# Moving the mixer's RMSNorm into FFN1 and handing its result over through DRAM

## The chip, the cores and the metric

One Trainium2 chip, eight cores. Each core works on its own two sequences (4096 tokens) with the same program; nothing is exchanged between cores. The time is that of one execution on the device, in microseconds, of the slowest core.

## What is computed

One decoder layer on x (16 x 2048 x 1024, float32), bf16 in the matmuls:

```python
x = x + 0.5 * swiglu(rmsnorm(x, ffn1_norm), ffn1_w_gate, ffn1_w_up, ffn1_w_down)   # FFN1
h = rmsnorm(x, mix_norm)                                                           # the norm that moves
q_lat, kv_lat, k_rope, xc, gB, gC, gate_logits = split(h @ w_in)
y_a = causal_block_attention(q, k, v) @ w_proj_attn     # q, k, v from the latents
y_b = (gB * conv3(gC * xc)) @ w_proj_conv
gates = sigmoid(gate_logits + gate_bias)
x = x + (gates[..., :D] * y_a + gates[..., D:] * y_b) @ w_out                      # mixer
x = x + 0.5 * swiglu(rmsnorm(x, ffn2_norm), ffn2_w_gate, ffn2_w_up, ffn2_w_down)   # FFN2
```

D = 1024, the FFN width is 2816, 8 heads, sequence length 2048.

## The kernel before

**Tiling.** Tokens go in eight groups (g = 0 to 7) of 512, each of four tiles of 128. All eight groups pass FFN1, then the mixer, then FFN2. Between the stages x lies in DRAM as float32: `x1_d` after FFN1, `x2_d` after the mixer. The matmuls want the normed activations transposed, channel in the partitions; `hT[0]` and `hT[1]`, used by even and odd groups, hold one group each in bf16.

**Streams and planner.** The program is written as streams (generators) that yield operations, each with an engine, what it reads and writes, and a booked cost. `FW.schedule` merges them: it emits next the operation whose estimated start is earliest; ties go to the stream that stands earlier in the list. The order so found is fixed for each engine's queue, and engines execute in order. For a DMA it books 2 us plus the size at 310 bytes per ns (`DMA_FIX`, `DMA_RATE`), one after the other on SP; DMAs of other queues are not counted against it. `Wait` holds a stream back until a flag is set by a `Do` of another; flags are set when operations are emitted, not when they execute. All plain loads, stores and transposes are issued by SP; the casts of weights from float32 to bf16 in DRAM (`cast_w`, L853 and L863) by POOL.

**The norm.** `norm_stream` (L869 on) is used three times, for FFN1 (`f1`), the mixer (`m`) and FFN2 (`f3`). Per tile: a load to one of two `xin` buffers (L883), ACT's Square with a running sum (L901), two small POOL operations for the power -0.5 (L903, L905), DVE's multiply by the factor and the gain row `grow` into `xn` (L907), and a transposing DMA from `xn` to `hT` (L918). The load of tile n+1 is issued before tile n is normed. FFN1's first group is transposed by PE instead (L914).

**Gates.** FFN1's norm of group g (g of 2 or more) waits for `f1.gu.{g-2}`, the last gate/up matmul that reads the same hT. The mixer's norm loads tiles once FFN1's own norms are all emitted; group g of 0 and 1 waits for `f1.gu.{6+g}`, a later group for `d.h.{g-2}` (the last matmul of group g-2 that reads hT, in `proj`) and `m.q.{g-2}` (its latents). The norm buffers, the gain row and the DMA queue of SP are shared by the three uses.

**FFN1.** `ffn_stream`: for each group 22 pairs of gate and up matmuls (8 matmuls of 512 columns each), Silu on ACT (L957), product on DVE (L959), in rotation over four PSUM banks; then the down-projection of four tiles (L739 is the helper line of every matmul), the residual on DVE, the store to `x1_d` (L993) and the load of the next group's residual (L937). `f1.g.{g}` is set when the last of these is emitted. In group 0 all four tiles of the down-projection end together.

**Mixer.** Three streams run side by side: `m_stream` (latents, q, k, v of group g: `qkv`), `a_stream` (attention of group g) and `d_stream` (convolution, projections and output of group g: `conv`, `proj`, `outp`), the last with ten ring buffers of weights (`ring_stream`, L1240). `m.n.{g}` says that hT holds group g; `qkv(g)` and `conv(g)` wait for it.

Of the kernel before, what the change touches and what calls it, by code (L numbers as in the profile page):

```python
# [454 lines left out]
def c_stt(n):  # L455
    return 215.0 + n * 1.042
# [14 lines left out]
def build_program():  # L471
# [101 lines left out]
    def ffn_bufs(tag):  # L573
# [26 lines left out]
        for i in range(2):  # L600
            xr.append(mk(f"{tag}xr{i}", [D], F32, a, 2))
            a = xr[-1].end
        assert a <= HI, (a, HI)
        f.all = f.gu + f.sg + [f.act] + [f.wd] + xr
# [8 lines left out]
    commit_regs(f1.all)  # L613

# [85 lines left out]

    d_x1 = [[Dep(f"x1.{g}.{t}") for t in range(TPG)] for g in range(NG)]
    d_x2 = [[[Dep(f"x2.{g}.{t}.{h}") for h in range(2)] for t in range(TPG)] for g in range(NG)]
    d_out = Dep("out")
# [22 lines left out]
    s_tk = fw.new_dma_sem("tk")  # L726
    s_grow = fw.new_dma_sem("grow")
    s_set = [fw.new_dma_sem(f"set{i}") for i in range(5)]
# [12 lines left out]

    def ld_grow(i):
        return dma("sp", s_grow, lambda e: e.dma_start(out=grow.t[:], in_=row_d[0:1, i * D:(i + 1) * D].broadcast_to([128, D])),
                   [], grow.d, 128 * D * 4)

# [122 lines left out]

    def norm_stream(tag, src_d, srcdep, gi_, gate):  # L869
        work = [(g, tt) for g in range(NG) for tt in range(TPG)]  # L870
        first = tag == "f1"

        def xbuf(n):
            if first and n in (2, 3):
                ap, dd = f1.xr[n - 2]
                return ap, dd, s_xr[n - 2]
            return xin[n % 2].t[:], xin[n % 2].d, s_xin[n % 2]

        def load(n):
            g, tt = work[n]  # L880
            ap, dd, sem = xbuf(n)
            r0 = g * G + tt * 128
            return dma("sp", sem, lambda e: e.dma_start(out=ap, in_=src_d[r0:r0 + 128, :]), srcdep(g, tt), dd, 128 * D * 4)  # L883

        nl = 0
        yield Wait(gate(0, "x"))
        if not first:
            yield ld_grow(gi_)
        for n, (g, tt) in enumerate(work):
            if tt == 0:  # L890
                yield Wait(gate(g, "h"))
            while nl < len(work) and nl <= (3 if first and n == 0 else n + 1):
                yield Wait(gate(work[nl][0], "x"))
                yield load(nl)
                if first and nl == 0:
                    yield ld_grow(gi_)
                nl += 1
            i = n % 2
            h = hT[g % 2]
            xa, xd, _ = xbuf(n)  # L900
            yield op("act", lambda e, i=i, xa=xa: e.activation(out=xn[i].t[:], in_=xa, func=AF.Square, scale=1.0 / 32.0,  # L901
                                                               accum_out=ssq.t[:, i, 0:1]), xd, [xn[i].d, ssq.d[i]], c_act(1024) + 190)
# [3 lines left out]
                                                            op=ALU.pow), [ssq.d[i], nhalf.d], [rr.d[i]], c_pow(1))  # L906
            yield op("dve", lambda e, i=i, xa=xa: e.scalar_tensor_tensor(out=xn[i].t[:], in0=xa, scalar=rr.t[:, i, 0:1], in1=grow.t[:],  # L907
                                                                         op0=ALU.mult, op1=ALU.mult),
                     [xd, rr.d[i], grow.d], xn[i].d, c_stt(1024))
# [10 lines left out]
            yield Do(lambda n_=f"{tag}.t.{g}.{tt}": flags.add(n_))  # L920
            if tt == TPG - 1:
                yield Do(lambda n_=f"{tag}.n.{g}": flags.add(n_))

# [514 lines left out]

    def gate3(g, what):
        if what == "x":  # L1440
# [3 lines left out]
        return lambda: f"f3.gu.{g - 2}" in flags  # L1444

    streams = [
        setup_a(),
        norm_stream("f1", x_d, lambda g, t: [], 0, gate1),
        norm_stream("m", x1_d, lambda g, t: [d_x1[g][t]], 1, gate2),
        norm_stream("f3", x2_d, lambda g, t: d_x2[g][t], 2, gate3),  # L1450
        a_stream(),
# [40 lines left out]
```

## Time and profile before

| | us |
|---|---|
| median of 3 runs | 3209.21 |
| lowest of them | 3209.09 |
| the profiled execution | 3209.18 |
| its span, slowest core | 3207.6 |
| spans of the eight cores | 3187.7 to 3207.6 |
| PE busy in the span | 3089.6 |

The span runs from the first to the last instruction of the slowest core. PE is TensorE's matmuls, PEld its weight loads, DVE VectorE, ACT ScalarE, POOL GpSimd, SP the queue that issues DMAs. L901 is line 901 of the kernel printed above. In a timeline a bracket holds the idle time of the engine just before an instruction, and what ended it. A landing is the time from the issue of a DMA to its completion.

### The profile page before, as it was taken

To read this page: it belongs to the slowest core of one execution; us is meant where nothing else is said; L and a number is where in the kernel's file an instruction comes from. 1 tells how busy PE (TensorE), PEld (TensorE's weight loads), DVE (VectorE), ACT (ScalarE), POOL (GpSimd) and SP (SyncE) were. 2 spreads that over 40 slices of the span, in tenths; PEclk is the share of its full clock that TensorE was granted. 3 is DMA by queue.
4 is the path that set the end of the run, shared out by engine and by line. 5 is a ranking of instruction groups with operands and counts; after the bars stand their busy time and mean duration, and the time that the engine had idled before them with its cause. 6 is when DMAs were issued, how large, how long until landed. Compare 5 with 4: busy or idle time off the path is not lost.

```text
span 3207.6 us, 41366 instructions; the slowest of 8 cores (3187.7 to 3207.6 us)
## 1 busy us (share of the span) xinstructions
PE 3089.6 (96%) x14432; PEld 1407.8 (44%) x14432; DVE 1135.7 (35%) x1592; ACT 926.1 (29%) x1766; POOL 671.3 (21%) x1120
## 2 busy tenths in 40 slices
PE   7899999999999889999999999999999999999999
PEld 3344444444444344444444444444444444444444
DVE  4322221221236454554655554534222222122111
ACT  4311111111124434546343446363211111111100
POOL 1000000000026544342545343531100000000000
PEclk9999999999999999999999999999999999999999
DMA  9996564554425474756575656557670331131010
GB/s 314 296 129 141 137 100 107 132 118 92 127 66 144 101 190 108 192 129 160 141 205 138 199 124 164 145 145 242 170 223 21 92 92 34 59 92 53 27 53 27
DMA packets 333478, 419.32 MB, mean 131 GB/s; under 512 B 204896, under 2 KB 213216, under 8 KB 329696
## 3 DMA queue, kind: packets, MB, share of 16 engines
q1 hardware_dynamic: 325360, 380.83, 43.0%
q0 software_dynamic: 7920, 35.85, 7.6%
q8 instruction: 124, 2.03, 0.3%
q14 instruction: 74, 0.61, 0.1%
HBM read 355.45 MB, written 86.64 MB: 138 GB/s over the span
## 4 chain that ended last, share of the span: by engine, by line
PE 87%; DMA 4%; POOL 4%; DVE 3%; issue 1%; ACT 1%; SPq 0%; ACTq 0%; DVEq 0%; POOLq 0%
PE banks L739 87%; POOL hr L1117 1%; DMA xin_69<-x1s 1%; DVE Rs L1206 1%; DMA axr_105<-ws 1%; POOL qf L1128 1%; DVE T_109 L1093 1%; DVE hs L1095 0%; POOL mrgT L1377 0%; DMA xin_69<-x 0%; DMA QT_120<-qf 0%; DVE xn_71 L907 0%; DMA QT_136<-qf 0%; POOL hq L1119 0%; POOL kf L1135 0%
## 5 line engine op out<-in xcount | busy, mean ns | idle before, releaser
L739 PE MATMUL banks<-awd,aact 128*128 128x512 bf16 x1408 | 306.7, 379 | 4.9 <-ACT awd L830 3.8
L739 PE MATMUL banks<-cwd,cact 128*128 128x512 bf16 x1408 | 305.2, 379 | 0.0
L903 POOL TENSOR_SCALAR ssq<-ssq 128x1 f32<-128x1 f32 x96 | 25.6, 266 | 919.1 <-ACT xn_70 L901 825.2
L739 PEld LDWEIGHTS banks<-awd,aact 128*128 128x128 bf16 x1408 | 137.3, 98 | 171.7 <-issue 7.4
L739 PEld LDWEIGHTS banks<-cwd,cact 128*128 128x128 bf16 x1408 | 137.9, 98 | 166.0
L957 ACT ACTIVATE csg_173<-banks 128x512 f32<-128x512 f32 x88 | 52.5, 597 | 425.9 <-PE banks L739 425.9
L957 ACT ACTIVATE asg_94<-banks 128x512 f32<-128x512 f32 x88 | 52.5, 597 | 388.0 <-PE banks L739 388.0
L959 DVE TENSOR_TENSOR cact<-csg_173,banks 128x512 bf16<-128x512 f32 x88 | 60.5, 687 | 236.7 <-PE banks L739 236.7
L959 DVE TENSOR_TENSOR aact<-asg_94,banks 128x512 bf16<-128x512 f32 x88 | 60.6, 688 | 235.3 <-PE banks L739 235.2
L959 DVE TENSOR_TENSOR cact<-csg_174,banks 128x512 bf16<-128x512 f32 x88 | 60.5, 687 | 234.5 <-PE banks L739 234.5
L959 DVE TENSOR_TENSOR aact<-asg_95,banks 128x512 bf16<-128x512 f32 x88 | 60.5, 688 | 230.2 <-PE banks L739 227.9
L1183 ACT ACTIVATE pt_123<-banks 128x512 bf16<-128x512 f32 (+2 forms) x216 | 116.0, 537 | 86.6 <-PE banks L739 80.3
L1183 ACT ACTIVATE pt_124<-banks 128x512 bf16<-128x512 f32 (+2 forms) x214 | 113.6, 531 | 56.7 <-PE banks L739 51.7
L1183 ACT ACTIVATE pt_125<-banks 128x512 bf16<-128x512 f32 (+3 forms) x210 | 110.3, 525 | 58.1 <-PE banks L739 55.5
L957 ACT ACTIVATE csg_174<-banks 128x512 f32<-128x512 f32 x88 | 52.5, 597 | 252.3 <-PE banks L739 252.3
L1206 DVE RECIPROCAL Rs<-Rs 128x128 f32<-128x128 f32 x128 | 121.3, 948 | 11.0 <-ACT Rs L1200 9.2
L957 ACT ACTIVATE asg_95<-banks 128x512 f32<-128x512 f32 x88 | 52.5, 597 | 241.2 <-PE banks L739 238.4
L1117 POOL TENSOR_TENSOR hr<-hm,nhalf 128x8 f32<-128x8 f32 x64 | 111.0, 1734 | 4.7
L1202 DVE COPY Xo<-banks 64x512 f32<-64x512 f32 x64 | 44.0, 688 | 150.4 <-PE banks L739 97.7
L907 DVE SCALAR_TENSOR_TENSOR xn_71<-xin_69,rr,grow 128x1024 bf16<-128x1024 f32 x47 | 62.5, 1331 | 55.8 <-POOL rr L905 44.5
L901 ACT ACTIVATE xn_70<-xin_68 128x1024 bf16<-128x1024 f32 x47 | 49.5, 1052 | 112.0 <-DMA xin_68<-x 52.6
L907 DVE SCALAR_TENSOR_TENSOR xn_70<-xin_68,rr,grow 128x1024 bf16<-128x1024 f32 x47 | 62.8, 1335 | 51.9 <-POOL rr L905 37.0
(479 smaller groups left out, 5610.4 us busy)
## 6 DMA issues: line engine op xcount, KB each, us to landing
wms<-ws POOLq DMA_DIRECT2D x33, 512.0 KB, 5.0
ring_127<-wms SPq DMA_DIRECT2D x52, 256.0 KB, 3.1
ring_129<-wms SPq DMA_DIRECT2D x51, 256.0 KB, 3.2
ring_131<-wms SPq DMA_DIRECT2D x51, 256.0 KB, 3.0
ring_133<-wms SPq DMA_DIRECT2D x51, 256.0 KB, 3.0
ring_135<-wms SPq DMA_DIRECT2D x51, 256.0 KB, 3.1
ring_126<-wms SPq DMA_DIRECT2D x39, 256.0 KB, 3.3
ring_128<-wms SPq DMA_DIRECT2D x39, 256.0 KB, 3.5
```

The lines of the kernel that those rows point to most:

```text
L739: fns.append(lambda e, o_=o_, l_=l_, r_=r_, st=st, sp_=sp_: e.matmul(o_, lhsT=l_, rhs=r_, start=st, stop=sp_))
L901: yield op("act", lambda e, i=i, xa=xa: e.activation(out=xn[i].t[:], in_=xa, func=AF.Square, scale=1.0 / 32.0, accum_out=ssq.t[:, i, 0:1]) ...
L903: yield op("pool", lambda e, i=i: e.tensor_scalar(out=ssq.t[:, i, 1:2], in0=ssq.t[:, i, 0:1], scalar1=EPS, scalar2=1.0, op0=ALU.add, op1=A ...
L907: yield op("dve", lambda e, i=i, xa=xa: e.scalar_tensor_tensor(out=xn[i].t[:], in0=xa, scalar=rr.t[:, i, 0:1], in1=grow.t[:], op0=ALU.mult ...
L957: yield op("act", lambda e, s_=s_, b0=b0: e.activation(out=s_.t[:], in_=bk(b0), func=AF.Silu), [d_bank[b0]], s_.d, c_act(512))
L959: pend = op("dve", lambda e, s_=s_, b1=b1, c=c: e.tensor_tensor(out=f.act.t[:, c, :], in0=s_.t[:], in1=bk(b1), op=ALU.mult), [s_.d, d_bank ...
L1093: yield op("dve", lambda e: e.tensor_tensor(out=T1, in0=q2, in1=CQ.t[:, tt, None, :].broadcast_to([128, NH, 128]), op=ALU.mult), [d_bank[B ...
L1117: yield op("pool", lambda e, jj=jj: e.tensor_tensor(out=hr.t[:, b, jj], in0=hm.t[:, b, jj], in1=nhalf.t[:, 0:8], op=ALU.pow), [hm.d[dj], n ...
L1128: yield op("pool", lambda e: e.tensor_tensor(out=qf.t[:], in0=T1, in1=hq.t[:, b, 0:8, None].broadcast_to([128, NH, 128]), op=ALU.mult), [T ...
L1183: yield op("act", lambda e: e.activation(out=p_.t[:, 0:w], in_=bk(b0)[:, 0:w], func=AF.Exp, scale=sc), [d_bank[b0]], p_.d, c_act(w))
L1202: yield op("dve", lambda e: e.tensor_copy(out=X.t[po:po + 64, :], in_=bk(OB)[po:po + 64, :]), [d_bank[OB]], X.d, c_dve(512))
L1206: yield op("dve", lambda e, qs=qs: e.reciprocal(out=R.t[:, qs], in_=R.t[:, qs]), R.d, R.d, 80 + 6.4 * 128)
```

## The change

The mixer's norm becomes part of FFN1's norm stream. After FFN1's norm of group g+2 follow the four mixer tiles of group g: the x1 tile is loaded, normed with a gain row of its own (`grow2`), and the bf16 result is stored to a new DRAM tensor `h1_d` in place of the transpose. The mixer tiles of the last two groups follow at the end of the list. A new stream, `turn_stream`, waits for a group's norms to be emitted and for hT to be free (the old gates), and issues four transposing DMAs from `h1_d` to `hT`, each with a semaphore of its own. Mixer loads are gated by `f1.g.{g}`. Since the load of tile n+1 is yielded before tile n is normed, the fourth FFN1 tile of group g+2 also comes behind that gate. FFN2's norm stays as it was.

```diff
+    h1_d = nc.dram_tensor("h1s", [TOK, D], BF16).ap()
...
+        if tag == "a":
+            f.grow = mk("grow2", [D], F32, a)
...
-    def norm_stream(tag, src_d, srcdep, gi_, gate):
-        work = [(g, tt) for g in range(NG) for tt in range(TPG)]
+    def norm_stream(work, gate):
...
-            while nl < len(work) and nl <= (3 if first and n == 0 else n + 1):
-                yield Wait(gate(work[nl][0], "x"))
+            while nl < len(work) and nl <= (3 if startup and n == 0 else n + 1):
+                yield Wait(gate(work[nl][0], work[nl][1], "x"))
                 yield load(nl)
-                if first and nl == 0:
-                    yield ld_grow(gi_)
+                if startup and nl == 0:
+                    yield ld_grow(grow, 0)
+                if startup and nl == 4:
+                    yield ld_grow(grow2, 1)
                 nl += 1
...
-            if first and g == 0:
+            if tag == "m":
+                r0 = g * G + tt * 128
+                yield dma("sp", s_tx[i], lambda e, i=i, r0=r0: e.dma_start(out=h1_d[r0:r0 + 128, :], in_=xn[i].t[:]),
+                          xn[i].d, [d_h1[g][tt]], 128 * D * 2)
+            elif startup and g == 0:
...
+    def turn_stream(gate):
+        for g in range(NG):
+            yield Wait(lambda g=g: f"m.s.{g}" in flags)
+            yield Wait(gate(g))
+            for tt in range(TPG):
+                r0 = g * G + tt * 128
+                yield dma("sp", s_th[4 * (g % 2) + tt], lambda e, g=g, tt=tt, r0=r0: e.dma_start_transpose(
+                    out=hT[g % 2].t[:, :, tt * 128:(tt + 1) * 128], in_=h1_d[r0:r0 + 128, :]),
+                    [d_h1[g][tt]], [d_hT[g % 2][tt]], 128 * D * 2)
+            yield Do(lambda n_=f"m.n.{g}": flags.add(n_))
...
-    def gate1(g, what):
+    def gate1(tag, g, what):
+        if tag == "m":
+            return lambda: f"f1.g.{g}" in flags
         if what == "x":
             return lambda: "seta" in flags
         return lambda: g < 2 or f"f1.gu.{g - 2}" in flags
 
-    def gate2(g, what):
-        if what == "x":
-            return lambda: f"f1.g.{g}" in flags and f"f1.n.{NG - 1}" in flags
+    def gate2(g):
         if g < 2:
             return lambda: f"f1.gu.{NG - 2 + g}" in flags
         return lambda: f"d.h.{g - 2}" in flags and f"m.q.{g - 2}" in flags
...
+    tiles = range(TPG)
+    work1 = []
+    for g in range(NG + 2):
+        if g < NG:
+            work1 += [("f1", g, tt) for tt in tiles]
+        if g >= 2:
+            work1 += [("m", g - 2, tt) for tt in tiles]
...
-        norm_stream("f1", x_d, lambda g, t: [], 0, gate1),
-        norm_stream("m", x1_d, lambda g, t: [d_x1[g][t]], 1, gate2),
-        norm_stream("f3", x2_d, lambda g, t: d_x2[g][t], 2, gate3),
+        norm_stream(work1, gate1),
+        turn_stream(gate2),
+        norm_stream(work3, gate3),
```

## Rows read from the trace of the kernel before

**Rows 1.** The page: busy us of each engine; granted clock in 40 slices.

```profile
PE 3089.6 (96%) x14432; PEld 1407.8 (44%) x14432; DVE 1135.7 (35%) x1592; ACT 926.1 (29%) x1766; POOL 671.3 (21%) x1120
...
PEclk9999999999999999999999999999999999999999
```

**Rows 2.** Stages: length; PE, PEld, DVE, ACT, POOL busy; clock; DMA; GB/s.

```profile
0.00:153.00 153.00, 124.20 (x560) 54.53 (x560) 64.29 (x95) 61.37 (x82) 13.18 (x31) 0.98 1.01 311
153.00:960.00 807.00, 806.52 (x3742) 366.71 (x3743) 190.45 (x260) 129.32 (x233) 69.58 (x133) 1.00 0.56 116
960.00:1127.00 167.00, 148.48 (x699) 68.28 (x697) 95.53 (x137) 73.51 (x156) 100.33 (x154) 0.94 0.52 122
```

**Rows 3.** The same view: the six stretches in which mixer norms run.

```profile
1127.00:1167.00 40.00, 33.20 (x151) 15.26 (x150) 18.85 (x28) 19.45 (x43) 13.97 (x27) 0.87 0.97 231
...
1311.00:1351.00 40.00, 35.34 (x170) 16.32 (x169) 23.62 (x35) 19.47 (x45) 14.40 (x28) 0.96 0.87 226
...
1478.00:1518.00 40.00, 34.69 (x168) 16.37 (x167) 19.50 (x29) 24.76 (x57) 12.69 (x27) 0.96 0.88 215
...
1638.00:1678.00 40.00, 34.41 (x167) 15.89 (x165) 25.94 (x39) 16.41 (x39) 18.84 (x35) 0.91 0.94 246
...
1800.00:1840.00 40.00, 36.84 (x175) 16.87 (x174) 25.99 (x39) 14.96 (x36) 14.44 (x30) 0.96 0.92 259
...
1962.00:2002.00 40.00, 34.75 (x177) 16.52 (x175) 22.46 (x31) 24.55 (x56) 14.75 (x30) 1.00 0.86 231
```

**Rows 4.** The same view: the six stretches between and after them.

```profile
1167.00:1311.00 144.00, 135.79 (x642) 62.29 (x641) 69.33 (x100) 67.76 (x136) 61.71 (x98) 0.98 0.47 121
...
1351.00:1478.00 127.00, 125.25 (x601) 57.89 (x599) 60.29 (x88) 62.24 (x121) 53.92 (x80) 1.00 0.51 134
...
1518.00:1638.00 120.00, 117.26 (x568) 54.32 (x567) 65.39 (x95) 49.18 (x98) 59.55 (x91) 1.00 0.53 140
...
1678.00:1800.00 122.00, 116.01 (x562) 53.80 (x561) 65.70 (x93) 53.15 (x107) 58.08 (x90) 1.00 0.55 143
...
1840.00:1962.00 122.00, 117.57 (x559) 54.03 (x557) 56.47 (x83) 58.45 (x115) 56.12 (x82) 0.99 0.47 122
...
2002.00:2138.00 136.00, 131.73 (x624) 60.25 (x623) 65.87 (x93) 65.88 (x128) 55.72 (x84) 0.99 0.47 124
```

**Rows 5.** Timeline of the first norm in the mixer: start, us, instruction.

```profile
1127.65 0.38 SPq L883 DMA_DIRECT2D xin_69<-x1s  x1
...
1136.35 1.06 ACT L901 ACTIVATE xn_71<-xin_69 128x1024 bf16<-128x1024 f32 x1 [4.34 <-DMA xin_69<-x1s]
...
1138.12 0.48 PE L739 MATMUL banks<-QT_136,KT_137 128*128 128x384 bf16 x1 [4.27 <-ACT pt_124 L1183]
```

**Rows 6.** POOL's casts; SP's tile load at 172.78, its landing; a median landing.

```profile
168.93 1.12 POOL L853 DMA_DIRECT2D wms<-ws  x2 [43.35 <-ACT asg_95 L957]
...
172.78 0.53 SPq L883 DMA_DIRECT2D xin_69<-x  x1
...
DMA to landing us min/median/max: 31.9/31.9/31.9
...
xin_69<-x1s SPq DMA_DIRECT2D x16, 512.0 KB, 5.5
```

**Rows 7.** Timeline of ACT: a Silu beside gate/up; a Square beside down-projection.

```profile
178.40 0.60 ACT L957 ACTIVATE asg_94<-banks 128x512 f32<-128x512 f32 x1 [2.86 <-PE banks L739]
...
249.98 1.06 ACT L901 ACTIVATE xn_70<-xin_68 128x1024 bf16<-128x1024 f32 x1 [17.12 <-DMA xin_68<-x]
```

**Rows 8.** Page groups, multiply and Square: busy us, mean ns | idle before.

```profile
L907 DVE SCALAR_TENSOR_TENSOR xn_71<-xin_69,rr,grow 128x1024 bf16<-128x1024 f32 x47 | 62.5, 1331 | 55.8 <-POOL rr L905 44.5
...
L901 ACT ACTIVATE xn_70<-xin_68 128x1024 bf16<-128x1024 f32 x47 | 49.5, 1052 | 112.0 <-DMA xin_68<-x 52.6
```

**Rows 9.** Line 918, transposes: ns min/median/max on SP; landings of all 92.

```profile
L918 SPq DMA_TRANSPOSE hT_67<-xn_70 x24: 1216/1218/6082, 37.3 to 2949.5; - x24
...
DMA to landing us min/median/max: 3.1/4.0/14.1
```

More of the change, by code:

```diff
@@ L602, in ffn_bufs @@
             a = xr[-1].end
+        if tag == "a":
+            f.grow = mk("grow2", [D], F32, a)
+            a = f.grow.end
         assert a <= HI, (a, HI)
@@ L612, in build_program @@
             dp.until = f"f1.gu.{NG - 1}" if b in f1.gu else "f1.done"
-    commit_regs(f1.all)
+    grow2 = f1.grow
+    grow2.d[0].until = f"m.s.{NG - 1}"
+    commit_regs(f1.all + [grow2])
     m = Buf()
@@ L701, in build_program @@
     d_x1 = [[Dep(f"x1.{g}.{t}") for t in range(TPG)] for g in range(NG)]
+    d_h1 = [[Dep(f"h1.{g}.{t}") for t in range(TPG)] for g in range(NG)]
     d_x2 = [[[Dep(f"x2.{g}.{t}.{h}") for h in range(2)] for t in range(TPG)] for g in range(NG)]
@@ L726, in build_program @@
     s_tk = fw.new_dma_sem("tk")
-    s_grow = fw.new_dma_sem("grow")
+    s_grow = [fw.new_dma_sem(f"grow{i}") for i in range(3)]
+    s_th = [fw.new_dma_sem(f"th{i}") for i in range(8)]
     s_set = [fw.new_dma_sem(f"set{i}") for i in range(5)]
@@ L867, in build_program, with src @@
     xc_ = {}
-    def norm_stream(tag, src_d, srcdep, gi_, gate):
-        work = [(g, tt) for g in range(NG) for tt in range(TPG)]
-        first = tag == "f1"
+    def norm_stream(work, gate):
+        def src(n):
+            tag, g, tt = work[n]
+            r0 = g * G + tt * 128
+            if tag == "f1":
+                return x_d[r0:r0 + 128, :], []
+            if tag == "m":
+                return x1_d[r0:r0 + 128, :], [d_x1[g][tt]]
+            return x2_d[r0:r0 + 128, :], d_x2[g][tt]
+        startup = work[0][0] == "f1"
         def xbuf(n):
-            if first and n in (2, 3):
+            if startup and n in (2, 3):
                 ap, dd = f1.xr[n - 2]
@@ L879, in load @@
         def load(n):
-            g, tt = work[n]
             ap, dd, sem = xbuf(n)
-            r0 = g * G + tt * 128
-            return dma("sp", sem, lambda e: e.dma_start(out=ap, in_=src_d[r0:r0 + 128, :]), srcdep(g, tt), dd, 128 * D * 4)
+            sap, sd = src(n)
+            return dma("sp", sem, lambda e: e.dma_start(out=ap, in_=sap), sd, dd, 128 * D * 4)
         nl = 0
-        yield Wait(gate(0, "x"))
-        if not first:
-            yield ld_grow(gi_)
-        for n, (g, tt) in enumerate(work):
+        yield Wait(gate(work[0][0], 0, "x"))
+        if not startup:
+            yield ld_grow(grow, 2)
+        for n, (tag, g, tt) in enumerate(work):
             if tt == 0:
-                yield Wait(gate(g, "h"))
-            while nl < len(work) and nl <= (3 if first and n == 0 else n + 1):
-                yield Wait(gate(work[nl][0], "x"))
+                yield Wait(gate(tag, g, "h"))
+            while nl < len(work) and nl <= (3 if startup and n == 0 else n + 1):
+                yield Wait(gate(work[nl][0], work[nl][1], "x"))
                 yield load(nl)
-                if first and nl == 0:
-                    yield ld_grow(gi_)
+                if startup and nl == 0:
+                    yield ld_grow(grow, 0)
+                if startup and nl == 4:
+                    yield ld_grow(grow2, 1)
                 nl += 1
@@ L1437, in gate2, with gate3 @@
         return lambda: f"d.h.{g - 2}" in flags and f"m.q.{g - 2}" in flags
-    def gate3(g, what):
+    def gate3(tag, g, what):
         if what == "x":
```

19 lines of the change are left out of this document (11 added, 8 removed).

## Prediction

> **What bounds the kernel now.** The page's busy table comes first: PE is busy for 3089.6 of 3207.6 us, in 14432 matmuls [rows 1]. Whatever the change takes from other engines counts only where PE stands still or is slowed, so the second view is the stage table [rows 2]. FFN1 after its start-up (153 to 960 us) has no hole: 806.52 of 807 us, and 806.52 / 3742 = 0.2155 us a matmul. The start-up has 28.8 us of PE idle while the DMA engines are full (share 1.01). The passage into the mixer, 960 to 1127, loses 18.5 us idle, and its clock of 0.94 costs another 0.06 x 167 = 10 us.
>
> The third view is the same table for the mixer, cut at the places where it now does its norm. Tokens go in groups of 512, and the norms of groups 2 to 7 run when hT becomes free, at about 1127, 1311, 1478, 1638, 1800 and 1962 us [rows 3]; between them lie the six stretches of [rows 4]. I price a stretch as idle time plus (1 - clock) x length: a granted clock of 0.87 is a mean of 2.4 and 1.2 GHz. The six clusters lose 12.0, 6.3, 6.9, 9.2, 4.8 and 5.3 us, together 44.4. The stretches between lose 32.9 us in 771, or 1.7 per 40 us, so ordinary loss would be 10.2 and the excess at the norms is 34 us.
>
> The fourth view, the timeline of the first cluster, shows a mechanism [rows 5]. The load of an x1 tile is issued at 1127.65; ACT, which executes in order, stands at Square (L901) for 4.34 us until it has landed; the exponentials of attention stand behind Square, and PE waits 4.27 us for one of them. The excess is therefore mostly a queueing effect, not the 1.05 us of Square or the 1.33 us of the DVE multiply [rows 8].
>
> **What the change removes.** In the mixer go the x1 loads, Squares, POOL steps and DVE multiplies of groups 2 to 7: 24 tiles. I take 60 to 65% of the 34 us as gone, 22 us, since the same moments also contain the end of an attention head, merge adds on POOL and the first latent projections, which stay. Bounds: all 34, and 10 (about the waits like that of [rows 5], if the rest is merely re-timed).
>
> **What it adds in the mixer.** Per group four transposes from DRAM follow each other on SP: 4 x 1.22 = 4.9 us of issue [rows 9], against four transposes and four loads spread out between the norms now. Behind them wait the weight loads of the ring, which has ten buffers of at most eight matmuls, 1.7 us each [rows 2], so about 15 us ahead; I cost the block at nothing, and at up to 5 us a group if the ring has run low. hT must only be ready for the next latent projections, which cannot start before it in either kernel.
>
> No transpose from DRAM is in this trace. The nearest rows are the same instruction from SBUF, landing after 4.0 us (up to 14.1) [rows 9], and a 512 KB load from x1, 5.5 us [rows 6]. From both sides: 4 us a tile as from SBUF, or 14.1 x 4 = 56 us a group if each costs the worst seen. I take about 5, nearer the load; that is earlier than today's hT, whose loads alone need about 4 x 5.5 us, two tiles at a time. At 56 us the ring would run dry, a rival below. On this price the Trainium skill (Advanced Engine Details and Errata, X-Bar Transpose (TRN2)) says transposing DMAs are as fast as regular ones, which speaks against that rival; no run here shows it for a DRAM source. By it the sum is the same, and only that rival's chance is smaller.
>
> **What it adds in FFN1.** 32 loads from x1, 32 Squares, POOL pairs, multiplies and 32 bf16 stores join FFN1. By engine time this is nothing: PE sets the pace, a Silu of 0.60 us comes every 3.45 us [rows 7], and ACT and DVE are free between. What counts is the place. Today FFN1's own norms run in the down-projections, when no Silu is due: at 249.98 ACT had waited 17.12 us for a load [rows 7], and PE lost nothing. In the changed order the tile after f1(g+2, 2) may go on only when the first mixer tile's load is out, and that waits for f1.g.g, the end of the down-projection. So f1(g+2, 3) and four mixer tiles run beside the gate/up matmuls, where ACT is in PE's loop. PE has four PSUM banks there: if a Silu can't run, PE does three more sets of eight matmuls, 3 x 8 x 0.2155 = 5.2 us, and then stops.
>
> For most groups a 512 KB load of 5.5 us is 1 to 2 us later than the planner books (2 us plus 512 KB at 310 B/ns, 3.7 us), inside those 5.2 us: cost nothing, 2 us in all for groups 1 to 6.
>
> Group 0 is different. Its flag comes just before 172.78, when SP has issued the last residual load (L937). The next load in this slot is, today, issued at 172.78 and takes 31.9 us [rows 6], since POOL has issued two large weight casts at 168.93 [rows 6] that share the DMA engines. Today that tile's Square is due only in the next down-projection. In the changed kernel the same slot holds the first x1 tile of the mixer, and its Square is placed among the Silus by the planner's 3.7 us plus queue, about 5 us after issue, near 178. ACT then stands until 172.8 + 31.9 = 204.7. The next Silu would start about 1.7 us after 178 (half a period), and PE stops 5.2 us later, at 185; it goes on after Square and Silu at 204.7 + 1.2 + 0.6 = 206.5. That is 21.5 us of PE idle. Afterwards the clock is low for a while; the first cluster, after a 4.27 us hole, lost 5.2 us by its 0.87 clock [rows 3, 5], so I add 4.5: 26 us. The casts wait for FFN1's progress, so they pause with PE and the following tiles load quickly. Bounds: 0 if the tile lands before Silus matter, 45 if two more tiles are late.
>
> The second gain row costs 512 KB in the start-up, where DMA is full: 0.524 MB / 311 GB/s = 1.7 us [rows 2]; the deferred f1(2,3) transpose gives some back. I take 1.
>
> **What moves into the passage.** m(6,3) and m(7,0..3) need f1.g.7, so five norms land after about 955, beside the first head of qkv(0), conv(0)'s copies on ACT, and, on SP, ahead of the ring's first loads. Group 1's four norms leave the down-projection before it. A cluster's four tiles have an excess of 34/6 = 5.7 us; for five, less some 2 us that an earlier qkv(0) gains: 5 us. Bounds 0 and 12.
>
> **Sum.** -22 (clusters) + 26 (group 0 in FFN1) + 2 (other groups) + 1 (gain row) + 5 (passage) = +12 us. The profiled execution took 3209.18 us, with 1.6 us around its span of 3207.6, and the median of the runs is 3209.21, so the two are one: 3209 + 12 = 3221 us, 0.4% slower.
>
> **Rivals.**
> *A: the wait in FFN1 is hidden, 3195 us.* If the group 0 tile lands soon, or Square stands late enough among the Silus, the 26 is about 2 and the rest gives -22 + 2 + 2 + 1 + 3 = -14. For it: loads elsewhere in FFN1 land in 5 us. Against it: the slot is the very one that took 31.9 us. It decides below about 10 us of landing (5 booked plus 5.2 of banks). With all 34 us gained as well: 3182. The Trainium skill (DMA: Bandwidth & Descriptors, Rules for kernel authors) says fixed DMA cost overlaps when a transfer is issued early and waited for late; by that rule the moved norm is hidden, which is this rival. Here the issue is early by one tile only, and the 31.9 us landing speaks against it.
> *B: the stalls are larger and the gain smaller, 3250 us.* Group 0 at 40, passage 10, other groups 4, clusters -14, gain row 1: +41. For it: several mixer tiles follow each other while casts run. Against it: casts stop when PE stops.
> *C: transposes from DRAM are slow, 3280 us or more.* At 56 us a group, less the ring's 15 us of lead and overlapped partly by the attention work that needs no ring, some 12 us of PE idle a group: 6 x 12 = 72 on top of what remains. It decides from about 20 us a group. Against it: nothing in the rows suggests more than a load's time.
> *D: faster by over 2%.* It would need 64 us; the 34 us of excess plus the whole 28.5 of the passage are 62.5. Nearly excluded.
> That the change does not do what it says has no room: each norm step of the mixer is issued elsewhere by the code.
>
> **Chances.** Forecast 0.50, A 0.28, B 0.15, C 0.05, D 0.02. The forecast's own range is 3206 to 3238. To leave out no more than 2 in 10, the range must take in A with its full gain and B: 3182 to 3255. A measurement of this kernel tells about 2% from no change, 64 us; forecast, A and B all lie inside: within 2% 0.92, slower 0.06, faster 0.02.
>
> **What would show it.** In the profile after: a Square of an x1 tile near 178 to 205 us with an ACT wait above 15 us and a PE hole of about 20 us beside it (the forecast), or none (A). Clusters at hT's release without Squares, their loss down from 44 to about 22. The passage at some 33 instead of 28.5 us. Transposes from DRAM landing in 4 to 6 us; above 15 is C. Holes of several us in the gate/up stages of later groups mean B. The forecast is wrong if the planner's new order puts a long wait where no row of today has one.

## The result, and the profile after

The changed kernel takes 3247.01 us (median of four executions, 3237.69 to 3253.93) against 3209.21 us for the kernel before in the same session (median of three; a fourth, of 3738.0 us in a slow state of the chip, is left out, as such executions are throughout). The ratio of the means is 1.0113, with a 95% interval of 1.0079 to 1.0146. It is 1.1% slower, 36 us, inside the 2% that the forecast calls no change, inside the range, and 26 us above the predicted 3221. For some of the experiments below too few executions were left for an interval; there the profiled execution stands alone.

The profiled execution took 3237.69 us, its slowest core (core 1) 3235.8. The page answers to [rows 1]: the same matmuls, the time lost elsewhere.

```profile
span 3235.8 us, 41381 instructions; the slowest of 8 cores (3202.7 to 3235.8 us)
PE 3080.0 (95%) x14432; PEld 1405.8 (43%) x14432; DVE 1135.4 (35%) x1592; ACT 926.8 (29%) x1766; POOL 663.8 (21%) x1120
```

Its chain of waits, by engine and item, now holds loads of x1 tiles:

```profile
PE 83%; DMA 7%; DVE 4%; POOL 2%; SPq 1%; issue 1%; ACT 1%; ACTq 0%; DVEq 0%; POOLq 0%
PE banks L747 82%; DMA xin_69<-x1s 2%; DMA xin_68<-x1s 1%; SPq L951 1%; POOL hr L1149 1%; DVE Rs L1238 1%; DVE T_110 L1125 1%; DVE hs L1127 0%; POOL qf L1160 0%; DMA cs_119<-css 0%; DMA cs_118<-css 0%; DMA css<-dscr_64 0%; DMA QT_121<-qf 0%
```

The stage table of the kernel after, cut as in [rows 2] but shifted by the later FFN1 (columns as there):

```profile
153.00:1004.00 851.00, 801.92 (x3681) 361.19 (x3679) 213.50 (x277) 147.13 (x265) 80.28 (x166) 0.97 0.59 131
1004.00:1172.00 168.00, 145.72 (x686) 65.97 (x685) 100.26 (x139) 69.50 (x151) 101.61 (x159) 0.94 0.53 136
```

Before, FFN1 had no hole and a clock of 1.00. Now this core idles for 49 us in it, at a mean clock of 0.97. The passage loses 22.3 us idle and 0.06 x 168 = 10 us of clock, 32.4 together, against 28.5 before and "some 33" forecast.

**The first hole.** Four timelines of the kernel after, core 1, around 175 to 230 us. POOL's casts:

```profile
175.15 1.12 POOL L861 DMA_DIRECT2D wms<-ws  x2 [48.71 <-ACT asg_95 L989]
183.76 0.57 POOL L861 DMA_DIRECT2D wms<-ws  x1 [3.50 <-DVE aact L991]
221.81 0.58 POOL L861 DMA_DIRECT2D wms<-ws  x1 [2.28 <-DVE aact L991]
```

SP's queue, and the landing of the x1 load issued at 178.68:

```profile
178.31 0.33 SPq L969 DMA_DIRECT2D dscr_65<-x  x1
178.68 0.69 SPq L898 DMA_DIRECT2D xin_68<-x1s  x1
181.69 23.88 SPq L940 DMA_TRANSPOSE hT_66<-xn_71  x1
205.66 1.65 SPq L898 DMA_DIRECT2D xin_69<-x1s  x1
...
DMA to landing us min/median/max: 33.9/33.9/33.9
```

ACT (L919 is Square, L989 the Silu):

```profile
184.62 0.60 ACT L989 ACTIVATE asg_94<-banks 128x512 f32<-128x512 f32 x1 [2.86 <-PE banks L747]
212.73 1.06 ACT L919 ACTIVATE xn_70<-xin_68 128x1024 bf16<-128x1024 f32 x1 [27.51 <-DMA xin_68<-x1s]
228.28 1.06 ACT L919 ACTIVATE xn_71<-xin_69 128x1024 bf16<-128x1024 f32 x1 [6.19 <-DMA xin_69<-x1s]
```

PE:

```profile
214.50 5.49 PE L747 MATMUL banks<-hT_67,agu_81 128*128 128x512 bf16 x16 [21.41 <-ACT asg_95 L989]
230.06 1.89 PE L747 MATMUL banks<-hT_67,agu_84 128*128 128x512 bf16 x8 [3.06 <-ACT asg_94 L989]
```

Read them together. The first x1 tile is asked for at 178.68, right behind the two casts of 175.15, and is there 33.9 us later. ACT stands at its Square for 27.51 us; the next Silu is behind it; PE fills its banks and then stands for 21.41 us. This is the mechanism and nearly the size (21.5 us) that the forecast worked out from [rows 6, 7].

**The later holes.** The same engines of the kernel after in the gate/up stage of the third group (g = 2). POOL goes on casting:

```profile
311.35 0.58 POOL L861 DMA_DIRECT2D wms<-ws  x1 [3.50 <-DVE aact L991]
323.00 0.58 POOL L861 DMA_DIRECT2D wms<-ws  x1 [2.29 <-DVE aact L991]
342.15 0.58 POOL L861 DMA_DIRECT2D wms<-ws  x1 [2.46 <-DVE aact L991]
```

SP asks for an x1 tile beside them, ACT waits for it, PE waits for ACT; the last line is the same one group later:

```profile
322.56 1.50 SPq L898 DMA_DIRECT2D xin_69<-x1s  x1
...
337.64 1.06 ACT L919 ACTIVATE xn_71<-xin_69 128x1024 bf16<-128x1024 f32 x1 [8.43 <-DMA xin_69<-x1s]
...
339.41 3.15 PE L747 MATMUL banks<-hT_66,agu_80 128*128 128x512 bf16 x7 [8.36 <-ACT asg_94 L989]
...
466.36 4.00 PE L747 MATMUL banks<-hT_67,agu_80 128*128 128x512 bf16 x9 [7.99 <-ACT asg_94 L989]
```

That tile landed some 15 us after its issue (322.56 to 337.64), where the forecast had taken 5.5. It was one of the latest: over the eight cores the median landing of an x1 tile in the stages of groups 2 and 3 is 5.9 and 8.2 us, and in those of groups 4 to 6 it is 5.5 to 6.0, though POOL casts there too. What counts is the longest. In the stage of group 2, cores 1 and 4, where a tile took 14.9 and 15.7 us, have holes of 8.4 and 6.7 us; the four cores whose tiles all landed within 6.5 us have none.

**The mixer.** The six stretches of 40 us from the turn of hT on, answering to [rows 3]:

```profile
1193.00:1233.00 40.00, 38.66 (x203) 19.22 (x201) 24.53 (x40) 20.47 (x50) 18.76 (x35) 1.00 0.85 192
1358.00:1398.00 40.00, 36.80 (x189) 17.94 (x188) 20.24 (x35) 14.99 (x39) 16.88 (x30) 1.00 0.75 180
1527.00:1567.00 40.00, 36.10 (x178) 17.38 (x177) 13.88 (x25) 21.85 (x51) 10.07 (x22) 0.96 0.61 153
1681.00:1721.00 40.00, 36.48 (x187) 17.76 (x186) 24.05 (x40) 10.85 (x30) 17.71 (x32) 1.00 0.88 223
1837.00:1877.00 40.00, 35.13 (x169) 16.83 (x168) 21.76 (x37) 9.12 (x26) 16.09 (x26) 0.96 0.93 216
2008.00:2048.00 40.00, 36.05 (x178) 17.39 (x176) 20.53 (x37) 9.22 (x28) 15.59 (x26) 0.96 0.88 220
```

Priced as before, idle plus (1 - clock) x 40, they lose 1.3, 3.2, 5.5, 3.5, 6.5 and 5.6 us, together 25.6 against 44.4; the forecast had about 22 left. The transposes from DRAM, source line 951:

```profile
L951 SPq DMA_TRANSPOSE hT_66<-h1s x16: 1216/1274/2996, 860.8 to 1842.5; - x16
L951 SPq DMA_TRANSPOSE hT_67<-h1s x16: 1216/1276/2571, 974.8 to 2012.5; - x16
...
  PE banks L747: 8.3, 5
...
DMA to landing us min/median/max: 3.5/4.8/7.1
```

They land in 4.8 us (about 5 forecast) and PE waited for them 8.3 us in five places (3.4 to 8.3 us on the eight cores).

**Where the time went.** For a comparison free of the choice of a core, the traces are cut on every core at four instructions (on DVE the first product of group 1's gate/up and FFN1's last product, on ACT the first Exp and FFN2's first Silu), and the lengths are averaged over the eight cores of the profiled execution, in us. The expectations below use the same marks; where they say "FFN1" they mean the second column, and "mixer part" is the third and fourth together.

| kernel | to group 1 | FFN1, rest | to first Exp | mixer | FFN2 | span, mean | slowest |
|---|---|---|---|---|---|---|---|
| before | 160.9 | 756.3 | 83.0 | 1199.8 | 997.6 | 3197.5 | 3207.6 |
| after | 162.3 | 797.1 | 90.2 | 1172.4 | 998.1 | 3220.1 | 3235.8 |
| e1_mixer_half | 178.5 | 756.3 | 82.9 | 1170.4 | 997.7 | 3185.8 | 3197.5 |
| e2_ffn1_half | 164.4 | 804.9 | 82.7 | 1183.5 | 998.0 | 3233.4 | 3255.7 |
| e3_casts_later | 162.8 | 776.8 | 91.5 | 1172.4 | 997.9 | 3201.4 | 3212.4 |
| e4_in_down | 164.6 | 762.5 | 92.8 | 1173.2 | 997.8 | 3191.0 | 3201.0 |
| e5_from_residual | 177.1 | 762.6 | 87.2 | 1170.0 | 998.4 | 3195.4 | 3211.1 |
| e6_reordered | 162.6 | 756.3 | 82.2 | 1197.5 | 998.5 | 3197.2 | 3212.3 |
| e6_reordered_b | 165.0 | 756.3 | 82.0 | 1201.3 | 998.5 | 3203.1 | 3211.7 |
| e7_norms_cut | 164.5 | 756.3 | 82.2 | 1186.9 | 997.8 | 3187.6 | 3194.7 |
| e8_group0_late | 167.6 | 757.6 | 87.9 | 1171.0 | 998.0 | 3182.3 | 3190.7 |
| e9_loads_cut | 165.9 | 756.8 | 82.5 | 1175.1 | 998.0 | 3178.5 | 3192.7 |

After against before: +1.4 + 40.8 + 7.2 - 27.4 + 0.5 = +22.5 us on the mean core, +28.2 on the slowest. Over all four executions of the changed kernel the mean core takes 3225.6 us. In the first column a few us can't be told from chance: before and the four kernels of experiments 4 and 5, which all have before's start-up, lie between 160.9 and 165.9. The third and fourth columns are best read together too, since the first Exp moves against the work around it: together they are 1282.8 us before and 1262.6 after, 20.2 less. Cut once more at each group's first product, FFN1 before takes 114.0 us a group; after, groups 1 to 6 take 140.2, 116.9, 123.0, 115.3, 115.0 and 114.2. So group 1 costs +26.2, and the other groups +14.4 on the mean core (they sum up to the 40.8 within rounding). On core 1 the others cost 25.3, on core 0 only 5.1: the cores differ in how late the tiles of groups 2 and 3 come.

### The profile page after: what moved, and what is told of

Read it like the earlier page. It is cut to its first block, busy times and chain, and to the rows that moved or that the text cites. A ratio compares the mean times of both kernels' runs of the same rounds, so it can differ in the third digit from the quotient of the medians.

```text
span 3235.8 us, 41381 instructions; the slowest of 8 cores (3202.7 to 3235.8 us)
## 1 busy us (share of the span) xinstructions
PE 3080.0 (95%) x14432; PEld 1405.8 (43%) x14432; DVE 1135.4 (35%) x1592; ACT 926.8 (29%) x1766; POOL 663.8 (21%) x1120
## 4 chain that ended last, share of the span: by engine, by line
PE 83%; DMA 7%; DVE 4%; POOL 2%; SPq 1%; issue 1%; ACT 1%; ACTq 0%; DVEq 0%; POOLq 0%
PE banks L747 82%; DMA xin_69<-x1s 2%; DMA xin_68<-x1s 1%; SPq L951 1%; POOL hr L1149 1%; DVE Rs L1238 1%; DVE T_110 L1125 1%; DVE hs L1127 0%; POOL qf L1160 0%; DMA cs_119<-css 0%; DMA cs_118<-css 0%; DMA css<-dscr_64 0%; DMA QT_121<-qf 0%; DMA QT_137<-qf 0%; DMA xin_68<-x2s 0%
## 5 line engine op out<-in xcount | busy, mean ns | idle before, releaser
L989 ACT ACTIVATE csg_174<-banks 128x512 f32<-128x512 f32 x88 | 52.5, 597 | 430.6 <-PE banks L747 427.1
L989 ACT ACTIVATE asg_94<-banks 128x512 f32<-128x512 f32 x88 | 52.4, 595 | 394.6 <-PE banks L747 390.0
L989 ACT ACTIVATE csg_175<-banks 128x512 f32<-128x512 f32 x88 | 52.5, 597 | 251.2 <-PE banks L747 251.2
L989 ACT ACTIVATE asg_95<-banks 128x512 f32<-128x512 f32 x88 | 52.4, 596 | 196.5 <-PE banks L747 193.4
L919 ACT ACTIVATE xn_70<-xin_68 128x1024 bf16<-128x1024 f32 x47 | 49.5, 1053 | 132.9 <-DMA xin_68<-x2s 46.2
L919 ACT ACTIVATE xn_71<-xin_69 128x1024 bf16<-128x1024 f32 x47 | 49.4, 1052 | 79.0 <-DMA xin_69<-x1s 53.6
L1405 DVE SCALAR_TENSOR_TENSOR dscr_65<-dscr_65,banks 128x512 f32<-128x512 f32 x32 | 22.0, 687 | 125.4 <-PE banks L747 123.8
```

The lines of the kernel that those rows point to most:

```text
L989: yield op("act", lambda e, s_=s_, b0=b0: e.activation(out=s_.t[:], in_=bk(b0), func=AF.Silu), [d_bank[b0]], s_.d, c_act(512))
L1405: yield op("dve", lambda e, sb_=sb_, b2=b2: e.scalar_tensor_tensor(out=sb_, in0=sb_, scalar=1.0, in1=bk(b2), op0=ALU.add, op1=ALU.mult), [ ...
```

## The experiments

**1. One half of the change each.** The theory: the norms in FFN1 cost by a late tile in front of the Silus, and the mixer gains what its norms cost. First the mixer's half: `h1_d` is filled with FFN1's own normed tiles, so the mixer works on those, and FFN1 norms nothing more.

```diff
+            if tag == "f1":
+                yield dma("sp", s_h1[i], lambda e, i=i, r0=r0: e.dma_start(out=h1_d[r0:r0 + 128, :], in_=xn[i].t[:]),
+                          xn[i].d, [d_h1[g][tt]], 128 * D * 2)
...
-        if g >= 2:
-            work1 += [("m", g - 2, tt) for tt in tiles]
```

> The mixer's half of the change alone. FFN1 does not norm x1 at all: the bf16 tiles stored to the DRAM tensor are FFN1's own normed tiles, so the mixer works on another norm's result (that part of the computation is left out); the four transposes per group from DRAM and all the rest of the mixer are those of the changed kernel, and FFN1 keeps 32 bf16 stores but loses the 32 x1 loads and Squares. Theory (the loss is made in FFN1 by Squares that stand on ACT until x1 tiles land; the mixer gains): FFN1 ends within 8 us of before (about 970 us instead of 1000 to 1028), the mixer stays near 1210 us instead of 1231, time about 3190 us, 0.994 of before. Rival (transposes from DRAM or the new SP order cost the mixer as much as the norms did): time 3205 to 3215, ratio 1.00.

Measured: 0.9968 of before (0.9948 to 0.9988). FFN1 is unharmed (756.3), the mixer takes 1170.4, 29.4 less than before and within 2 us of after. The 17.6 us in the first column are this experiment's own: its stores of the first tiles fall into the start-up, where the DMA engines are full [rows 2]. The first store lands after 21.1 us, the third tile needs its buffer, and PE waits 20.59 us for that tile (2.07 in before).

Then FFN1's half: groups 0 to 5 are normed and stored in FFN1 as in the changed kernel, and the mixer norms all groups again as before, from `x1_d`.

```diff
-        if g >= 2:
-            work1 += [("m", g - 2, tt) for tt in tiles]
+        if 2 <= g:
+            work1 += [("m", g - 2, tt) for tt in tiles if g - 2 < 6]
+    workm = [("M", g, tt) for g in range(NG) for tt in tiles]
...
-        turn_stream(gate2),
+        norm_stream(workm, gatem),
```

> FFN1's half alone. FFN1 loads, norms and stores the mixer tiles of groups 0 to 5 as in the changed kernel, but nobody reads them; the mixer makes its own norms from x1 with transposes from SBUF, as before. Theory: FFN1 ends at 1000 to 1028 us as in the changed kernel (some 30 to 60 us later than before), the mixer takes 1225 to 1240 us as before, time about 3255 us, ratio 1.014 or more. Rival (the loss belongs to the hand-over, the last two groups' norms in the passage, or to DRAM transposes): FFN1 ends within 15 us of before and the time is below 3225.

Measured: 3257.24 us in the profiled execution (3257.87 in another); no interval. FFN1 loses 48.6 us, with PE's holes where after has them, one of them larger. PE's timeline of this kernel:

```profile
217.01 12.18 PE L747 MATMUL banks<-hT,agu 128*128 128x512 bf16 x48 [22.64 <-ACT asg L991]
...
469.02 11.17 PE L747 MATMUL banks<-hT,agu 128*128 128x512 bf16 x42 [7.86 <-ACT asg L991]
```

So the FFN1 half alone makes the loss, and the passage (82.7) is as before, since here the last groups' norms don't press into it. But the mixer, which norms all its tiles again, is 16.3 us shorter than before. That was expected by neither theory, and raised a doubt: is after's shorter mixer the removed work, or only the other order that the planner writes out? Experiments 4 and 5 take it up.

**2. What the first wait hangs on.** Two ways to take away what ACT waits for. Later casts (the first one eight products later, FFN2's 24):

```diff
-            at = 22 + 3 * i
+            at = 30 + 3 * i
...
-            at = 86 + 2 * i
+            at = 110 + 2 * i
```

> The changed kernel with POOL's weight casts started 8 gate/up chunks (about 28 us) later, nothing else; the two large ones no longer meet the first x1 tile. Theory (that tile is late because the casts share the DMA engines): its load lands in 5 to 12 us instead of 33, ACT's wait of 27.5 us before its Square and PE's hole of 21.4 us beside it go, FFN1 ends 15 to 30 us earlier than in the changed kernel unless the next groups meet casts instead, time 3215 to 3230. Rival (the extra work of ACT and DVE in FFN1, or the new order itself, holds PE): PE still has a hole of more than 15 us in group 1 and the time stays at 3240 to 3255.

Measured: 1.0039 of before (1.0015 to 1.0063). Only half of FFN1's 40.8 us is gone (776.8 in place of 797.1). The timelines of ACT and of PE show the wait halved, not removed: the first three tiles now land in time, and the fourth of the same stage meets the casts (it landed after 15.2 to 19.8 us on the eight cores).

```profile
211.48 1.06 ACT L919 ACTIVATE xn<-xin 128x1024 bf16<-128x1024 f32 x1 [15.88 <-DMA xin<-x1s]
...
213.25 32.00 PE L747 MATMUL banks<-hT,agu 128*128 128x512 bf16 x138 [10.81 <-ACT asg L989]
```

The other way: the casts stay, and the norm of group g waits for the end of the next group's gate/up matmuls, so that it stands in a down-projection, where no Silu is due.

```diff
         if tag == "m":
+            if what == "h" and g < NG - 1:
+                return lambda: f"f1.gu.{g + 1}" in flags
             return lambda: f"f1.g.{g}" in flags
```

> The changed kernel with the mixer's norm of group g held back to the down-projection of group g+1, where no Silu is due; same loads, same casts, same work. Theory (only Squares that wait beside gate/up matmuls stop PE): the long ACT waits remain, but PE's holes in FFN1 after 160 us shrink from about 40 us to under 12, FFN1 ends at 970 to 985 us, time 3190 to 3205. Rival (more DMA traffic or engine work in FFN1 slows PE wherever the norms stand): FFN1 still ends 30 us or more later than before, time 3235 or more.

Measured: 3202.68 us in the profiled execution; no interval. FFN1's rest falls to 762.5. The tiles are late as before (the one issued at 212.05 landed after 49.9 us), and ACT waits long for it, but PE has one hole of more than 1 us left. Timelines of ACT, DVE (L925 is the norm's multiply, L1021 the residual add) and PE:

```profile
262.13 1.06 ACT L919 ACTIVATE xn<-xin 128x1024 bf16<-128x1024 f32 x1 [21.24 <-DMA xin<-x1s]
...
264.29 1.28 DVE L925 SCALAR_TENSOR_TENSOR xn<-xin,rr,grow 128x1024 bf16<-128x1024 f32 x1 [21.01 <-POOL rr L923]
265.49 1.41 DVE L1021 SCALAR_TENSOR_TENSOR axr<-banks,axr 128x512 f32<-128x512 f32 x2
...
266.32 8.86 PE L747 MATMUL banks<-awd,aact 128*128 128x512 bf16 x33 [6.49 <-DVE axr L1021]
```

The same 32 loads, Squares and stores, with the same casts beside them, cost 34.6 us less: the place among the Silus was the price, not the work. The hole that is left is the same fault on DVE: the late tile's multiply stands there ahead of the residual adds that free the banks.

**3. The norm without the load.** The residual tile that FFN1 has just finished is normed where it lies in SBUF, into a Silu buffer that is free then, so no x1 tile is loaded again.

```diff
+                if tag == "f1":
+                    for o_ in mix_norm(g, tt, x, xd):
+                        yield o_
...
-        if g >= 2:
-            work1 += [("m", g - 2, tt) for tt in tiles]
```

> The mixer's norm is taken from the residual tile while it still lies in SBUF, right behind the residual add: no x1 tile is loaded again in FFN1, and the Squares stand on ScalarE where the last Silu of the group is behind them. The theory of the stall (a Square in order ahead of Silus, waiting for a load that is late behind the casts): the 21 us hole of group 1 and the holes of 8 us in the third group go, FFN1 from the first product of group 1 to the last product is 756 to 764 us (before 756.3, after 797.1, mean of the cores), the mixer keeps after's length, and the time is about 3190 us, 0.994 of before (0.990 to 0.999). The rival, that 24 more norms cost FFN1 time by their engine work and by their stores wherever they stand: FFN1 stays over 780 and the time is that of before or more.

Measured: 0.9997 of before (0.9986 to 1.0009), not the 0.994 expected. From group 2 on no hole is left (114.0 us a group), but group 0 makes a new one, 16 us ahead of group 1 and 7 in it. The timelines of PE and of ACT (L1042 is the residual add, L1010 the Silu):

```profile
170.71 3.57 PE L748 MATMUL banks<-hT,agu 128*128 128x512 bf16 x8 [12.88 <-DVE dscr L1042]
...
196.63 18.57 PE L748 MATMUL banks<-hT,agu 128*128 128x512 bf16 x74 [12.86 <-ACT asg L1010]
...
195.89 1.08 ACT L1010 ACTIVATE asg<-banks 128x512 f32<-128x512 f32 x2 [18.05 <-DMA h1s<-asg]
```

Group 0's four tiles end together, so their residual adds and norms alternate on DVE while PE wants the banks; then a Silu needs the buffer whose store to `h1_d`, issued at 179.26, lands after 16.6 us beside a cast issued at 179.53. The stores of that line landed in 2.4 us in the median, and this one was the longest. A transfer waited for beside the casts, by ACT, is the same fault in another place.

The cure follows: group 0 alone goes back to the norm stream, in the seventh group's down-projection (the gate that puts it there, `f1.gu.6`, is left out below).

```diff
-                if tag == "f1":
+                if tag == "f1" and g > 0:
                     for o_ in mix_norm(g, tt, x, xd):
...
+    work1 += [("m", 0, tt) for tt in tiles]
```

> The norm from the residual tile, as in e5_from_residual, for groups 1 to 7; group 0, whose four residual tiles all end at once when PE waits for them (two holes of 12.9 us at 171 and 197 us there), is left to the norm stream with its x1 loads, in the seventh group's down-projection, long after the weight casts. If the late load in front of the Silus and these four tiles were all that the FFN1 half cost, the start to group 1's first product comes back from 177.1 to 161 to 165 us, FFN1 from there to its last product is 756 to 762, the mixer part stays at 1255 to 1262 (before 1282.8), and the time is about 3188 us, 0.993 of before (0.989 to 0.997). If 24 to 28 norms in FFN1 cost by their work and stores wherever they stand, FFN1 is over 770 and the time at least 0.998 of before.

Measured: 0.9921 of before (0.9887 to 0.9956), 3192.21 us in the profiled execution. FFN1's rest takes 757.6 us, 1.3 more than before, and the mixer keeps its gain (1171.0). With all norms of the mixer in FFN1 this version is faster than both kernels, by 0.8% than the kernel before. The first column is 6.7 us longer than before's, of which up to 5 us are within what before's own start-up shows. The one hole of PE at its end, for a residual add, is there in before too (4.66 us, at 153.48) and in after (4.32, at 160.17):

```profile
164.63 50.68 PE L748 MATMUL banks<-hT,agu 128*128 128x512 bf16 x224 [5.58 <-DVE dscr L1042]
```

**4. The mixer's gain: order or work?** The kernel before, with one figure of its planner changed (100 or 300 ns more for a Square of the mixer), which makes it write the mixer's instructions in another order, with the same work.

```diff
-                                                               accum_out=ssq.t[:, i, 0:1]), xd, [xn[i].d, ssq.d[i]], c_act(1024) + 190)
+                                                               accum_out=ssq.t[:, i, 0:1]), xd, [xn[i].d, ssq.d[i]], c_act(1024) + 190 + (100 if tag == "m" else 0))
```

> The kernel before with nothing changed but one figure of its planner: a Square of the mixer's norm is assumed 100 ns longer, so that the planner writes the mixer's instructions out in another order, the same work in all. From the first Exp to FFN2's first Silu, mean of the cores, before takes 1199.8 us, after 1172.4, and the run with the norms done twice 1183.5. If after's shorter mixer is the norms' work alone, this run takes 1196 to 1204; if a good part of it is only another order, the length moves by 8 us or more to either side. FFN1 stays at 756.

> The same with 300 ns, which gives another order again: a second sample. The norms' work alone: 1196 to 1204 us from the first Exp to FFN2's first Silu; the order: away from 1199.8 by 8 us or more, and not by the same as with 100 ns.

Measured: 1197.5 and 1201.3 us from the first Exp to FFN2's first Silu, against 1199.8. Two other orders moved the mixer by -2.3 and +1.5 us. Each is one execution, and on the mean core their spans (3197.2 and 3203.1) lie inside those of eleven executions of before (3196.5 to 3204.4), so no gain or loss is shown. Single stretches do move: from the norms of group 2 to those of group 3 (second x1 load to second x1 load) before takes 178.0 us on the mean core and the first reordering 166.8, but the next such stretch takes 178.9 in place of 168.2. In experiment 1's second kernel the two are 163.4 and 173.3, so most of its 16.3 us lie in a stretch that an order alone can shorten.

**5. The same order with less work.** The kernel before, its order kept to the instruction; Squares and multiplies of the mixer's norm on 64 columns of 1024 (a mixer Square then takes 0.254 us and a multiply, cut likewise, 0.344, against 1.05 and 1.33 in [rows 8]). In this kernel and in the next the other 960 columns of a tile are not normed; they are left from an earlier tile.

```diff
+            w = 64 if tag == "m" else D
...
-            yield op("act", lambda e, i=i, xa=xa: e.activation(out=xn[i].t[:], in_=xa, func=AF.Square, scale=1.0 / 32.0,
+            yield op("act", lambda e, i=i, xa=xa, w=w: e.activation(out=xn[i].t[:, 0:w], in_=xa[:, 0:w], func=AF.Square, scale=1.0 / 32.0,
```

> The kernel before with its order kept to the instruction, but each of the mixer's 32 Squares and normalizing multiplies works on 64 columns in place of 1024; the output is therefore not the reference's. x1 is still loaded and the tiles are still transposed out of SBUF. If the engine work of the norms makes the clusters dear, the stretch from the first Exp to FFN2's first Silu falls from 1199.8 by 15 to 25 us, time 0.993 to 0.996; if the transfers (x1 loads, transposes) or the order do, by less than 8 us, time 0.997 to 1.000.

Measured: 0.9956 of before (0.9940 to 0.9972); the mixer is 12.9 us shorter by the table (the next expectation says 12.4), between the two forecasts, so engine work is about half of it. Then the x1 loads too, on 64 columns:

```diff
-            return dma("sp", sem, lambda e: e.dma_start(out=ap, in_=src_d[r0:r0 + 128, :]), srcdep(g, tt), dd, 128 * D * 4)
+            return dma("sp", sem, lambda e: e.dma_start(out=ap[:, 0:w], in_=src_d[r0:r0 + 128, 0:w]), srcdep(g, tt), dd, 128 * D * 4)
```

> As e7_norms_cut (the order of before kept to the instruction, the mixer's Squares and multiplies on 64 columns, so the output is not the reference's), and x1 too is loaded for 64 columns only, 32 KB in place of 512 KB a tile. In e7 the time lost between the first Exp and FFN2's first Silu fell by 12.4 us of the 27 that after saves. If the x1 loads hold the rest, this run saves 22 to 30 us of the 1199.8 (time about 0.991); if the rest is the order of the instructions and the chain from a free hT to its transposes, it saves 11 to 16 us as e7 did (time 0.995 to 0.996).

Measured: 0.9907 of before (0.9874 to 0.9939); the mixer is 24.7 us shorter. The loads of this kernel, from the list of DMA issues (KB each, median us to landing), where [rows 6] has 512 KB and 5.5:

```profile
xin<-x1s SPq DMA_DIRECT2D x32, 32.0 KB, 3.2
```

With before's order, then, the engine work of the norms is worth 12.9 us and their loads, cut after it, 11.8 more, together 24.7, beside the 27.4 that the changed kernel saves. That part is shown, and so is its place: priced like [rows 3], six stretches of 40 us from those loads on lose on the mean core 38.9 us before, 25.9 in the first of these kernels and 14.4 in the second, while the rest of the mixer stays at 63 in all three. The changed kernel, with no norms there, still loses 23.5 in its six, from a group's first transpose on; the waits for its transposes from DRAM are a part of that. What is left open is experiment 1's second kernel: with all norms in its mixer it saved 16.3 us, which two reorderings did not show. A third order that hides most of the norms' cost is one reading, which fits the stretches of experiment 4; no run here tests it by itself.

## Why the prediction was right or wrong, point by point

The direction, the verdict within 2% and the range were right; the time, 3221, was 26 us low against the median. On the mean core the sum of +12 became +22.5: the other groups +12.4 over their term, the mixer -5.4, the passage +2.2, so that two misses pulled against each other. Most of the rest is the spread of executions and cores: the profiled execution, the fastest of four, is +28.5 on its like of before. (The lower end of the range should read 3183, not 3182: 3195 less the 12 between 22 and 34.)

**Group 0 in FFN1, +26 predicted.** Group 1's stage measured +26.2 on the mean core. PE's hole is 21.41 us (21.5 worked out; 20.6 on the mean core), its cause the one named, and experiment 2 shows it: another place for the Square removes the hole with loads just as late. The landing of 33.9 us agreed with the 31.9 of [rows 6]. That the whole came out at 26 is in part luck: the smaller holes behind it, which the forecast put at nothing, took 2.6 us on the mean core, and some 3 us are left for the low clock, where 4.5 were added. Rival A was the wait hidden. The Trainium skill says that the fixed setup cost overlaps when a DMA is issued early and its semaphore is waited for late (DMA: Bandwidth & Descriptors, Rules for kernel authors). Here a load issued one tile early was not hidden, and ACT waited 27.51 us in front of Silus; with the wait moved into a down-projection (experiment 2) ACT still waited 21.24 us, but FFN1's rest took 762.5 us in place of 797.1.

**Other groups, +2 predicted, +14.4 measured** (25.3 on the slowest core): the term that was mis-sized, and most of the miss. The step that failed was "For most groups a 512 KB load of 5.5 us", put "inside those 5.2 us: cost nothing", with its companion that casts "pause with PE and the following tiles load quickly". 5.5 us is a median over 16 loads of one buffer [rows 6], and all but one of them landed with no cast in flight. The casts do pause with PE (none between 183.76 and 221.81), but they come back with it and run on, and a tile issued beside them took up to 15.7 us. As a median 5.5 was not far off; it hid the long landings, and every hole of more than 1 us in the stages of groups 2 to 6 stands on a core where a tile took over 9 us. The trace of before had a nearer row. The Square at 249.98 of [rows 7], read there for PE losing nothing, waited for this load, issued behind two casts:

```profile
218.98 0.52 POOL L853 DMA_DIRECT2D wms<-ws  x1 [9.85 <-DVE aact L959]
229.34 0.52 POOL L853 DMA_DIRECT2D wms<-ws  x1 [9.84 <-DVE aact L959]
...
236.73 0.52 SPq L883 DMA_DIRECT2D xin_68<-x  x1
...
DMA to landing us min/median/max: 13.1/13.1/13.1
```

13.1 us is above the "about 10 us of landing" from which, by the forecast's own rival A, PE stops. The 31.9 us of [rows 6] is no price for these groups either: the first tile, behind the two large casts, took 29.3 to 33.9 us on the eight cores, and no later one more than 15.7. Why the holes shrink after group 3 is not tested; from group 4 on POOL casts the smaller pieces of FFN2's weights (512 KB written, against 768 KB and more). Rival B named this ("several mixer tiles follow each other while casts run") and was set aside by the pause.

**The mixer, -22 predicted, -27.4 measured** (with the passage in front of it -17 predicted and -20.2 measured). The forecast took 60 to 65% of an excess of 34 us; the runs show 24.7 for engine work and loads together at an unchanged order, and the clusters' loss fell from 44.4 to 25.6. What the forecast called mostly queueing behind a late load was half that: cutting the instructions with the loads kept gave 12.9.

**The passage, +5 predicted, +7.2 measured;** its loss by the stage table 32.4 us, as forecast. **The gain row, +1 predicted,** can't be told: the start is 1.4 us longer, less than the 5 us by which kernels with before's own start-up differ.

**Transposes from DRAM,** the term with the widest bounds: 4.8 us at a guess of 5, at most 7.1, so rival C did not come, though the block, put at nothing, left PE waits of 3.4 to 8.3 us a core. The Trainium skill's statement that transposing DMAs are as fast as regular ones (Advanced Engine Details and Errata, X-Bar Transpose (TRN2)) agrees roughly: 4.8 us for 256 KB against medians of 4.3 to 5.4 for plain loads of 256 KB from x1 in this kernel, but 2.9 to 3.9 for the ring's loads of that size.

So the arithmetic that was done with rows of the very same slot came out within a microsecond for the hole; the term that used a median from other moments, and left out the long landings, came out seven times too small.

## What to carry to other kernels

When work is moved into a stage with room on its engines, ask what each in-order queue holds behind the moved instruction, and price its load by rows of the same moment, beside the same other traffic, and by the longest of them, not by a median over the run. A wait is harmless where nothing of PE's loop stands behind it in any queue, so move the wait, or take the operand while it is still in SBUF; here the first gave 34.6 us back in FFN1, and the second together with one late group made the moved norm pay (0.9921 of before). To know what removed work was worth, shrink it in place with the order of instructions kept.

## What the runs showed of the hardware that was not expected

A transposing DMA can hold its issuer for long: the transpose at 181.69, issued behind the large casts and the late load, took 23.88 us to issue on SP (the median on that buffer is 1.22), and the next x1 load went out only at 205.66. On the eight cores it took 20.1 to 25.1 us; in the kernel with later casts (experiment 2) none took more than 9.8. What holds it is not shown. Stores beside casts can be late like loads: 16.6 us to land against a median of 2.4 in experiment 3. And the x1 loads were worth nearly as much as the engine work: made 16 times smaller, landing 2.3 us sooner, they shortened the mixer by 11.8 us, where cutting the Squares and multiplies had given 12.9.
